# Fp32 value and third gate projections in both mixers of a three-part transformer kernel

## The reference

```
h = rms_norm(x, norm1_g[l]) * (1.0 + scale1) + shift1
z = h @ w_in[l]                       # 1024 x 4608: q, k, v, ga, gb, gates
q, k, v = z[..., 0:512], z[..., 512:1024], z[..., 1024:1536]
o = diff_attention(rope(q), rope(k), v, lam)
y_attn = (rms_norm(o) * (1.0 - lambda_init)) @ w_attn_o[l]
ga, gb = split(z[..., 1536:2560], 2)
u = causal_depthwise_conv(ga * sigmoid(gb), dw_conv_w[l], dw_conv_b[l])   # 31 taps
y_conv = silu(layer_norm(u)) @ w_conv_o[l]
g_attn, g_conv = split(sigmoid(z[..., 2560:4608]), 2)
x = x + (1.0 + gate1) * ((g_attn * y_attn + g_conv * y_conv) @ w_out[l])
```

## Time and profile before

| | |
|---|---|
| median of 3 runs | 2473.92 us (2473.72 to 2474.51) |
| profiled execution, its own time | 2476.07 us |
| its span, first to last instruction | 2474.3 us |
| PE busy | 2368.3 us, 96% |
| DVE busy | 1938.3 us, 78% |
| ACT busy | 1416.3 us, 57% |
| mean granted clock of PE | 0.984 |

### The profile page before, as it was taken

One profiled execution on the slowest core, in us unless ns is written; L12 is line 12 of the kernel. 1 busy time (PEld: TensorE's weight loads), 2 busy tenths in 40 slices (PEclk: granted clock), 3 DMA queues, 4 the chain that ended last, 5 costly groups with the idle time before them and its releaser, 6 DMA issues.

```text
span 2474.3 us, 29798 instructions
## 1 busy us (share of the span) xinstructions
PE 2368.3 (96%) x11879; PEld 1979.0 (80%) x11879; DVE 1938.3 (78%) x1864; ACT 1416.3 (57%) x1408; POOL 17.4 (1%) x33
## 2 busy tenths in 40 slices
PE   4988999998999899899999989999999999999998
PEld 4866788867888898798888978888888888888886
DVE  6997878787797656675445769898989898989897
ACT  2654433645543454455434547777777777777776
POOL 0000000000000000000000000000000000000000
PEclk9999999999999999899999989999999999999999
DMA  9556889434598445345555439999999999999996
GB/s 339 190 180 240 314 299 345 147 136 153 186 334 299 149 154 188 125 166 185 189 193 184 155 123 365 357 360 353 360 353 360 352 363 351 364 352 358 352 362 222
DMA packets 434768, 652.93 MB, mean 264 GB/s; under 512 B 20144, under 2 KB 323888, under 8 KB 434624
## 3 DMA queue, kind: packets, MB, share of 16 engines
q1 hardware_dynamic: 432592, 644.63, 75.9%
q0 software_dynamic: 2032, 6.33, 0.8%
HBM read 649.82 MB, written 1.05 MB: 263 GB/s over the span
## 4 chain that ended last, share of the span: by engine, by line
PE 90%; DVE 6%; ACT 2%; issue 1%; DMA 1%; SPq 0%; ACTq 0%; DVEq 0%
PE pair L2019 27%; PE pair L2021 27%; PE pair L2020 27%; PE pair L2054 3%; PE tb L2230 2%; PE pair L2411 1%; DVE aw L1516 1%; DVE rest L1147 1%; PE pair L2142 1%; DMA raw<-in_ada_w 1%; PE tb L2097 1%; DVE gat L1166 1%; ACT aw L722 0%; PE pair L2155 0%; DVE hT L1266 0%
## 5 line engine op out<-in xcount | busy, mean ns | idle before, releaser
L1147 DVE TENSOR_TENSOR rest<-raw,head 128x2048 fp32r<-128x2048 f32 x542 | 1240.6, 2291 | 300.6 <-ACT head L693 285.1
L693 ACT ACTIVATE head<-raw 128x2048 fp32r<-128x2048 f32 x542 | 1035.7, 1912 | 340.3 <-PE pair L2021 300.6
L2019 PE MATMUL pair<-head,hTh 128*128 128x512 f32 x1848 | 739.2, 400 | 4.7 <-DVE rest L1147 2.2
L2021 PE MATMUL pair<-head,hTl 128*128 128x512 f32 x1848 | 723.0, 391 | 0.0
L2020 PE MATMUL pair<-rest,hTh 128*128 128x512 f32 x1848 | 722.2, 391 | 0.0
L2019 PEld LDWEIGHTS pair<-head,hTh 128*128 128x128 f32 x1848 | 348.6, 189 | 77.3 <-issue 7.0
L2021 PEld LDWEIGHTS pair<-head,hTl 128*128 128x128 f32 x1848 | 348.0, 188 | 74.0
L2020 PEld LDWEIGHTS pair<-rest,hTh 128*128 128x128 f32 x1848 | 349.0, 189 | 69.2 <-issue 1.2
L2019 PE MATMUL pair<-head,aTh 128*128 128x512 f32 x776 | 308.6, 398 | 4.9 <-issue 3.8
L2021 PE MATMUL pair<-head,aTl 128*128 128x512 f32 x776 | 304.2, 392 | 0.0
L2020 PE MATMUL pair<-rest,aTh 128*128 128x512 f32 x776 | 304.0, 392 | 0.0
(11 more groups left out here) (302 smaller groups left out, 1653.2 us busy)
## 6 DMA issues: line engine op xcount, KB each, us to landing
raw<-in_moe_w_gate SPq DMA_DIRECT2D x224, 512.0 KB, 5.3
raw<-in_moe_w_up SPq DMA_DIRECT2D x224, 512.0 KB, 7.1
raw<-in_moe_w_down SPq DMA_DIRECT2D x224, 512.0 KB, 5.8
raw<-in_w_in SPq DMA_DIRECT2D x152, 512.0 KB, 4.6
raw<-in_ada_w SPq DMA_DIRECT2D x96, 512.0 KB, 5.7
raw<-in_w_ffn_in SPq DMA_DIRECT2D x88, 512.0 KB, 5.6
raw<-in_w_ffn_out SPq DMA_DIRECT2D x44, 512.0 KB, 5.4
raw<-in_w_out SPq DMA_DIRECT2D x40, 512.0 KB, 4.5
```

Of the source, the lines that this page charges most:

```text
L693: act.activation(head[:, c.split, :], raw[:, c.raw, :], ACT.Copy).then_inc(heads_done, 1)
L1147: dve.tensor_tensor(rest[:, c.split, :], raw[:, c.raw, :], head[:, c.split, :].bitcast(F32), ALU.subtract).then_inc(rests_done, 1)
L2019: pe.matmul(out_, lh, rh, start=start, stop=False, skip_group_check=True)
L2021: return pe.matmul(out_, ll, rh, start=False, stop=stop, skip_group_check=True)
```

## The change

Two more projections of both mixers are made unsplit: v and gates.2. With gates.0 and gates.1 between them, eight chunks in a row of the chunk order are then unsplit. No engine's list of work is reordered; the heads, the rests and the waits follow from the plan.

```diff
         plan_rotate(l)
-        plan_linear(f"v{l}", w, 512, "act", 1024)
+        plan_linear(f"v{l}", w, 512, "act", 1024, unsplit=True)
         plan_scores(l)
         plan_linear(f"gates{l}.0", w, NT, "act", 2560, unsplit=True)
         plan_linear(f"gates{l}.1", w, NT, "act", 2560 + NT, unsplit=True)
         plan_apply(l)
-        plan_linear(f"gates{l}.2", w, NT, "act", 2560 + 2 * NT)
+        plan_linear(f"gates{l}.2", w, NT, "act", 2560 + 2 * NT, unsplit=True)
         plan.job(f"oturn{l}", "act")
```

## The result

The changed kernel takes 2485.24 us (median of 5, 2483.56 to 2487.18) against 2473.92 (median of 5, 2470.73 to 2475.55). The medians lie 11.3 us apart; the ratio is 1.0048 with an interval of 1.0037 to 1.0059, which is 9.2 to 14.6 us. The forecast was 2480.4, slower, with 2484.6 as its upper end. The sign was right, the size short by 4.8 us: 11.3 in place of 6.5.

The account below looks back on a forecast made before the run. PE was taken as almost without slack, with DVE setting a stretch of each mixer; 3.3 + 2.25 + 1.0 = 6.55 us against the median 2473.92 gave 2480.4 us, own range 2478.9 to 2482.4, 8 in 10 from 2475.6 to 2484.6.

Parts of the forecast that it names:

- The price of a chunk: PE in v and gates.2: 6.89 us per unsplit chunk, v 2.57 and gates.2 2.78 more, 5.35 per mixer.
- Rival D: PE's unsplit chunks: the fourth fp32 pass counts in full, 7.33 us a chunk, +3.6 on 2480.4, 2484; chance 0.02.
- DVE's and ACT's relief is worth nothing: Removed rests and head copies gain nothing; DVE's wait before the head scaling hides them, growing from 0.97 to 5 to 8.
- First mixer, +3.3 at the turn back: Later gates.3 delays ACT's hTh, DVE's rest and the channel norm; turn back of normed channels from 185.25 to 188.55.
- Second mixer, +2.25: Normed channels 3.26 later, but turn back only from 586.22 to 588.47, as PE's slow yattn.0 had set it before.
- Clock, +1.0: PE's half clock moves from yattn.0 to behind the turn back: 1.0 us in the first mixer, nothing in the second.
- DMA, costed at nothing: Raw buffers of v and gates.2 free later, second w_attn_o load at about 156.8; about 13 us cover a load.
- A (the relief pays): Mixers' ends: DVE is ready when PE ends gates.3, waits and slow clock vanish, -5.4, 2468.5; chance 0.04.
- B (the clock refunds): Turns back set by PE alone, yattn.0 at full clock, refunding most of the cost: +1.5, 2475.4; chance 0.16.
- C: More slow clock at second mixer's yattn.0, first turn back and a later drop: +10.6, 2484.5; chance 0.16.

Follow-up runs that it names:

- experiment 9: Changed kernel with two more conv taps on DVE before the head scaling; ratio 1.0039 (1.0026 to 1.0053) to the kernel before the change.
- Experiment 8: Changed kernel with the channel norm's mean moved forward on DVE, right after yattn.0's rest; ratio 1.0018 (1.0009 to 1.0027) to the kernel before the change.
- experiment 6: Kernel before the change with unused matmuls on PE, three before the channel turn, two before yattn.0; ratio 1.0013 (1.0004 to 1.0022) to it unedited.
- Experiment 5: Changed kernel with unused matmuls on PE before yattn.0 and the turn back; ratio 1.0038 (1.0025 to 1.0052) to the kernel before the change.
- experiments 1: Changed kernel run again without edit; 2484.63 us against 2474.39 for the kernel before the change, ratio 1.0041 (1.0027 to 1.0055).

## Why the prediction was wrong in size

- *The price of a chunk*: right. 6.9 us each, 2.61 (v, forecast 2.57) and 2.74 (gates.2, 2.78) more. Rival D, a chunk of 7.33 us, is out.
- *DVE's and ACT's relief is worth nothing*: right. The wait at L1529 is 6.42 us (forecast 5 to 8), and experiment 9 shows that using 3.3 us of it brings nothing. One reason given was misread. The rotation's arithmetic on DVE (L1551) did not wait for PE before the change, it stood behind v's rests and began 3.03 us behind PE's rotation; now it begins at 2.01 and waits 3.67 for PE. DVE then waits 2.72 us for the scores in front of the masks (L1564, at 114.89), where it had no wait before, so nothing follows from it.
- *First mixer, +3.3 at the turn back*: measured +3.56, by the steps named: PE, ACT's hTh, DVE's rest, yattn.0's rest, the mean. Experiment 8 shows that they hold it. Most of the quarter us more is v's later start, 3.46 us behind the first rotation matmul in place of 3.26.
- *Second mixer, +2.25*: **this term was too small.** The turn back did come 2.54 later than in the trace that the forecast was read from (90.00 against 87.46 behind the rotation), but it is not what PE waits for next. The step that failed is that the sum stopped at the turn back and let PE's slow yattn.0, which had made it late before, pay for a part of the shift. The channel norm goes on through ACT's silu and DVE's rest of the conv half, all 3.5 later, to yconv; the stretch to the merged turn grew by 3.54. The row of that rest (591.25), next to PE's yconv at 592.58, would have told. Nor was the slow yattn.0 a fixed part of the kernel before: in its second profile the turn back is at 86.43, and against that it moved by 3.57.
- *Clock, +1.0*: **too small as well, and the larger part of the miss.** The whole costs 10.2 to 11.3 by the medians, the two mixers' fixed stretches 7.1; 3 to 4 us are left where I had 1. In the first profile before, 6.8 us of half clock fell around and on each yattn.0; in the first mixer that cost nothing (experiment 6). Now drops fall partly behind the turn back, and cost, against 259.9 us before, 1.7, 3.5 and 0.0 us in the three profiled executions of the changed kernel and its variant with taps first, 1.7 in the mean, and 2.6 in that with the first mixer alone. Experiment 5 has 0.1 there and is 2.3 us shorter in all, inside its noise. The drop behind the second layer's norm adds 1.5 us in two of those three executions, 1.0 in the mean, and in neither profile of the kernel before. Here the forecast's reading failed too: it took 447.2 to 452.6 as a place that keeps the full clock, from one execution, and behind the same work half of all profiles fall to half clock. With both, the profiles hold 9.8 of the 10.2 to 11.3 us. But three executions against two don't measure a mean, and why more of the drops should fall on PE's path in the changed kernel stays open.
- *DMA, costed at nothing*: right. The second w_attn_o chunk was issued at 155.60 (forecast 156.8), and no head waited for it.
- *Rivals*: A (the relief pays) and B (the clock refunds) did not happen. C, at 2484.5, came nearest to the time, 2485.24. It named more half clock, and a second mixer of +3.3, but through a slow yattn.0; what held the second mixer was the conv half.

## What to carry to other kernels

Trading work of one engine for more on another pays only where the relieved engine is waited for behind the place of the relief and before its next wait. Here the eight subtractions end ahead of waits for the very engine that got the extra work. Follow a delayed chain past the first event at which two chains meet: an engine that gains slack at one wait may lose it at the next operand. Read such a meeting in more than one profile: one whose place moves with the clock is not a bound. And when a helper engine's list is in order, the cheapest gain may be a tiny instruction that stands behind large ones; here one of 0.16 us, moved forward, made the kernel before 0.15% faster.

## What the runs showed of the hardware

A half-clock stretch is not only a loss but a place: the same 3.4 to 6.8 us of it cost nothing beside another engine's chain and up to 3.5 us behind it (experiments 1, 5 and 6), and it moved between executions of one kernel: granted 0.83 from 176 to 186 in one profile of the changed kernel, 0.76 from 186 to 200 in the other. Filling PE's standstills with unused matmuls raised the mean granted clock from 0.985 to 0.986 or 0.987, and made the kernel before slower all the same, 1.0013 (1.0004 to 1.0022).
